# Attention's outputs turned and normalised on chip, V stored by pair, and a later sum of the experts in a hybrid encoder block

## The chip, the cores and the metric

The kernel runs on one core of one Trainium2 chip. The metric is the device time of one execution in microseconds (us), as the median of several runs; smaller is better. A profile comes from one further execution.

## The reference, cut to what matters

One layer over 1024 tokens of width 1024, all in float32. Tiles are 128 tokens, eight in all.

```python
n1 = modulate(h, norm1_g, sh1, sc1)
z, xbc, dtf, dtb, qkv, gate_ssd, gate_na = split(n1 @ w_in)
y_ssd = ssd_branch(z, xbc, dtf, dtb, ...) @ w_ssd_br
y_na = neighbourhood_attention(q, k, v, na_rpb) @ w_na_br
mixed = sigmoid(gate_ssd) * y_ssd + sigmoid(gate_na) * y_na
h = h + g1 * (mixed @ w_out)
n2 = modulate(h, norm2_g, sh2, sc2)
h = h + g2 * peer(n2, peer_wq, peer_keys, peer_u, peer_v)
return rms_norm(h, final_g)
```

The attention works on a grid of 16 rows of 64 tokens. A row's queries see 8 rows of keys (512 keys); 16 heads of 64 channels:

```python
s = einsum('qd,kd->qk', q, k) + bias      # 64 queries, 8 rows of keys, per head
o = einsum('qk,kd->qd', softmax(s), v)
```

`peer` picks for each token and each of 8 heads the 16 best of 16384 experts, which makes 128 rows of `peer_u` and 128 rows of `peer_v` (4 KB each) per token:

```python
act = gelu(einsum('thkd,td->thk', u[eidx], xc))
return einsum('thk,thkd->td', gate * act, v[eidx])
```

## The kernel before, in words

Every engine runs one fixed list of instructions, and semaphores tie the lists together. The stages are: the condition and the first norm, the projections (`stage_project`), v, z and gates (`stage_gates`), q and k (`stage_qk`), the recurrence (`stage_ssd`), and then `stage_tail`, which holds the rest: attention, the two branch products, the output product, the second norm, the queries and scores of the expert layer, and the expert layer itself.

`stage_tail` interleaves two things. The **stream** of the expert layer goes by slots, 128 per tile, one for each expert of each token: in slot n POOL fetches one row of `peer_u` for each of 128 tokens (512 KB, an indirect DMA, L2229) into a ring of 5 buffers, VectorE makes the dot product (L2397), and every 32 slots, a grain, make a unit: GELU (ScalarE, `GELU_AT`), weights (VectorE, L2346), a turn on TensorE (L2409), and a copy of the turned weights into the spread matrix `spread` (ScalarE, L2262). POOL also fetches the rows of `peer_v` (L2222, 512 KB each, a ring of 12 buffers), and TensorE sums them, four fetches a batch, with `spread` as weights into PSUM `acc` (L2443). A fetch into the ring of 12 waits for the sum three batches earlier. The constants `FETCH_AT` and `SUM_AT` say how many slots after a grain's end its fetches and sums begin.

The **lane** is the dense work. It runs in passes of two tiles; pass 0 comes before the stream, passes 1 to 3 are laid into the slots by a planner (`PE_COST` shares the slots, `GAP` leaves slots free ahead of a kind of job). A pass does, in this order: `gate` (loads `n1_scr`, six column blocks of `w_in`, L1680), `recur` (the recurrence), `attend`, `merge`, `prepare` (output product, second norm, queries, scores). Scores go to HBM, and SP loads them back `SCORES_LEAD` slots before the stream needs them (L2179).

`attend` handles 32 units in a pass (8 pairs of heads, 4 grid rows). A unit: scores of both heads in one product with a block-diagonal q (L1843), scale and bias (VectorE, L1945), row maximum (L1949), exp (ScalarE, L1878), four transposes on TensorE (L1860), copy to `PT` (ScalarE, L1872), four products with V (L1852), and a division by the row sums on the way out of PSUM (VectorE, L1960). The three parts of TensorE's work in one job belong to units `it`, `it - 2` and `it - 1`. The kept blocks go to HBM, `na_scr`, with 256-byte pieces (L1572), and are loaded back in `merge` and turned by TensorE before the product with `w_na_br`. V is loaded twice for each pair: once by tiles of 128 keys, once shifted by 64 keys, so that a unit whose window starts at an odd row finds its keys at partition 0:

```python
for b in range(4):
    last = nc.tensor.matmul(values_bank(a_pass, u), PT[:, u % 2, b, :],
                            V[:, p % RP, odd * nk + b0 + b, :], start=(b == 0), stop=(b == 3))
```

The names: `acc`, `ps_n2F`, `ps_l`, `ps_turn` are PSUM, `lane` and `ring` the shared SBUF areas, `lane<-n_scr` a load of `n1_scr`, `n<-n_scr` the load of `n2`.

## Time and profile before

| | us |
|---|---|
| median of 3 runs (4532.55 to 4545.38) | 4540.99 |
| the profiled execution, its own time | 4573.06 |
| its span | 4571.3 |
| first row of `peer_u` fetched | 1038.9 |
| last indirect fetch issued | 4552.1 |

Busy in the span: PE 2882.9, DVE 2629.4, ACT 777.6, POOL 2072.6. The 16 DMA engines moved 1443 MB. The profiled execution is 32 us longer than the median. A group of rows carries the time an engine was busy, the mean of one instruction, and the idle time just before it with what ended it. The DMA share is that of the time packets took, so it can exceed 1 a little.

### The profile page before, as it was taken

How to read it: one execution, taken by the hardware profiler on the slowest of the kernel's cores; microseconds unless marked ns; L12 is line 12 of the kernel's file. 1: busy time of each engine (PE TensorE's matmuls, PEld its weight loads, DVE VectorE, ACT ScalarE, POOL GpSimd, SP SyncE). 2: the span in 40 equal slices, each digit the busy share in tenths (PEclk: the TensorE clock that was granted, in tenths of full speed). 3: DMA queues.
4: the chain of work that ended last, by engine and by line, in shares of the span. 5: the costliest groups of instructions: out<-in, count | busy, mean ns of one | idle time of the engine just before them, and what ended most of it. 6: DMA issues, size and time to landing. Idle time of an engine off the chain costs nothing. (4 is left out here: it accounts for less than half of the span.)

```text
span 4571.3 us, 38523 instructions
## 1 busy us (share of the span) xinstructions
PE 2882.9 (63%) x12379; PEld 1502.5 (33%) x12379; DVE 2629.4 (58%) x5465; ACT 777.6 (17%) x1601; POOL 2072.6 (45%) x2154
## 2 busy tenths in 40 slices
PE   4989996895755666694466756944657573223334
PEld 3867775542222432331233223322332230000000
DVE  3862118427476756447677565467775656665652
ACT  3323222311122210111122101111221010000000
POOL 1000303004454455445645555456555556666665
PEclk8989998997877888897677878976778796555656
DMA  7544634448989999999999999989999999999998
GB/s 197 115 133 134 177 91 158 153 170 327 383 314 328 346 367 406 394 350 335 366 343 336 404 406 405 372 324 368 351 327 404 407 386 377 381 364 367 381 364 318
DMA packets 566934, 1442.97 MB, mean 316 GB/s; under 512 B 85416, under 2 KB 184720, under 8 KB 565712
## 3 DMA queue, kind: packets, MB, share of 16 engines
q0 software_dynamic: 298768, 1086.75, 63.5%
q1 hardware_dynamic: 267968, 353.77, 22.4%
q8 instruction: 101, 1.65, 0.1%
q14 instruction: 97, 0.79, 0.0%
HBM read 1364.96 MB, written 75.38 MB: 315 GB/s over the span
## 5 line engine op out<-in xcount | busy, mean ns | idle before, releaser
L2397 DVE CUSTOM_DVE_ANT_0 junkF<-ring,ps_n2F 128x1024 bf16<-128x1024 f32 x1024 | 1249.0, 1220 | 850.5 <-DMA ring<-in_peer_u,idx 568.3
L2229 POOL DMA_INDIRECT ring<-in_peer_u,idx x1024 | 983.7, 961 | 1251.3 <-DVE dots L2397 750.9
L2443 PE MATMUL acc<-ring,spread 128*32 128x512 f32 x4096 | 717.6, 817 | 913.1 <-DMA ring<-in_peer_v,idxT 681.8
L2222 POOL DMA_INDIRECT ring<-in_peer_v,idxT x1024 | 981.4, 958 | 551.5 <-issue 309.5
L1680 PE MATMUL ps_l<-lane 128*128 128x512 f32 x1856 | 864.1, 619 | 136.0 <-DMA lane<-n_scr 75.2
L2443 PEld LDWEIGHTS acc<-ring,spread 128*32 128x32 f32 x4096 | 146.7, 135 | 1375.7 <-issue 1289.5
L1680 PEld LDWEIGHTS ps_l<-lane 128*128 128x128 f32 x1856 | 355.7, 197 | 610.2 <-issue 579.0
L1852 PE MATMUL ps_l<-lane 128*128 128x128 f32 x768 | 146.4, 350 | 161.0 <-ACT lane L1872 125.5
L1852 PEld LDWEIGHTS ps_l<-lane 128*128 128x128 f32 x768 | 129.1, 251 | 241.7 <-ACT lane L1872 170.3
L1843 PE MATMUL ps_l<-lane 128*128 128x512 f32 x192 | 128.3, 756 | 81.3 <-DVE lane L1945 73.8
L717 POOL MEMSET colmask<- 128x64 f32 x1 | 0.2, 156 | 364.7 <-POOLq L604 364.7
L1723 PE MATMUL ps_l<-lane 128*128 128x512 f32 x96 | 83.2, 1017 | 100.5 <-DVE tok L1810 73.3
L1878 ACT ACTIVATE lane<-lane,nmax 128x512 f32<-128x512 f32 x96 | 69.3, 722 | 359.1 <-DVE nmax L1949 207.2
L1945 DVE SCALAR_TENSOR_TENSOR lane<-ps_l,lane 128x512 f32<-128x512 f32 x96 | 66.0, 687 | 90.6 <-DMA rpb_scr<-bias_pad 82.8
L773 DVE TENSOR_TENSOR w_qk_lo<-w_qk,w_qk_hi 128x1024 fp32r<-128x1024 f32 x16 | 24.9, 1558 | 153.6 <-ACT w_qk_hi L755 153.6
L567 PE MATMUL ps_x<-n_hi,w_x_hi 128*128 128x512 f32 x256 | 104.8, 409 | 11.3 <-DVE w_x_lo L447 11.3
L659 DVE TENSOR_TENSOR w_z_lo<-w_z,w_z_hi 128x512 fp32r<-128x512 f32 x64 | 40.7, 687 | 121.8 <-ACT w_z_hi L631 88.3
L567 PE MATMUL ps_qk<-n_hi,w_qk_hi 128*128 128x512 f32 x256 | 102.4, 400 | 9.9 <-DVE w_qk_lo L773 9.9
L2246 ACT ACTIVATE gatesF<-gatesF 128x16 f32<-128x16 f32 x64 | 13.2, 207 | 537.7 <-DVE gatesF L2330 318.1
L567 PE MATMUL ps_x<-n_lo,w_x_hi 128*128 128x512 f32 x256 | 103.1, 403 | 0.0
L567 PE MATMUL ps_x<-n_hi,w_x_lo 128*128 128x512 f32 x256 | 102.8, 402 | 0.0
L567 PE MATMUL ps_qk<-n_lo,w_qk_hi 128*128 128x512 f32 x256 | 102.2, 399 | 0.0
(327 smaller groups left out, 4054.0 us busy)
## 6 DMA issues: line engine op xcount, KB each, us to landing
lane<-in_w_in SPq DMA_DIRECT2D x18, 2048.0 KB
lane<-in_peer_wq SPq DMA_DIRECT2D x16, 2048.0 KB
adaB<-in_w_ada SPq DMA_DIRECT2D x16, 1024.0 KB
w_z<-in_w_in SPq DMA_DIRECT2D x16, 1024.0 KB
lane<-in_w_ssd_br SPq DMA_DIRECT2D x8, 2048.0 KB
lane<-in_w_na_br SPq DMA_DIRECT2D x8, 2048.0 KB
lane<-in_w_out SPq DMA_DIRECT2D x8, 2048.0 KB
ring<-in_peer_u,idx POOLq DMA_INDIRECT x1024
```

The costliest lines, as they stand in the source:

```text
L567: last = nc.tensor.matmul(bank, stationary(left, k), moving(right, k), start=(k == 0 and n == 0), stop=(k == KD - 1 and n == 2))
L659: nc.vector.tensor_tensor(parts[1][:, q % RP, :], w[:, k // KH, k % KH, :], parts[0][:, q % RP, :], ALU.subtract).then_inc(lo_done, 1)
L1680: last = nc.tensor.matmul(bank, inT[:, f % SETS, k, :], w[:, blk % RW, k, :], start=(k == 0), stop=(k == KD - 1))
L1723: nc.tensor.matmul(ps_a, masks[:, 2 + d, :], rhs[:, d, :, :].rearrange("p h n -> p (h n)"), start=(d == 0), stop=(d == 1))
L1843: nc.tensor.matmul(scores_bank(a_pass, u), qd[:, p % RP, i, :], kT[:, p % RP, k0:k0 + HALF], start=True, stop=True).then_inc(qk_done, 1)
L1852: last = nc.tensor.matmul(values_bank(a_pass, u), PT[:, u % 2, b, :], V[:, p % RP, odd * nk + b0 + b, :], start=(b == 0), stop=(b == 3))
L1878: nc.scalar.activation(S[:, u % 2, :], S[:, u % 2, :], ACT.Exp, bias=nmax[:, u % 2:u % 2 + 1], accum_out=rsum[:, u % 4:u % 4 + 1]).then_in ...
L1945: nc.vector.scalar_tensor_tensor(out=S[:, u % 2, :], in0=scores_bank(a_pass, u), scalar=HEADDIM ** -0.5, in1=bias[:, p % RP, s0:s0 + NA_KH ...
L2222: pool.indirect_dma_start(v_rows[:, nv % RV, :], None, a["peer_v"][0], bass.IndirectOffsetOnAxis(ap=idxT[:, m % 2, col:col + 1], axis=0)). ...
L2229: pool.indirect_dma_start(u_rows[:, n % RU, :], None, a["peer_u"][0], bass.IndirectOffsetOnAxis(ap=idx[:, i % RI, j:j + 1], axis=0)).then_ ...
L2397: nc.vector.tensor_tensor_reduce(out=junk[:, :], in0=u_rows[:, n % RU, :], in1=ps_n[:, :], scale=1.0, scalar=0.0, op0=ALU.mult, op1=ALU.ad ...
L2443: last = nc.tensor.matmul(acc[q * QUAD:(q + 1) * QUAD, cols], spread[:, c0:c0 + QUAD], v_rows[:, nv % RV, cols], start=(g == 0 and b == 0) ...
```

## The change

1. Attention's turn is a product with `diag`, the identity times the reciprocal of the row sums (made by VectorE one unit earlier than the division was), instead of a transpose with the identity. The product with V has V as the stationary operand, so it comes out turned; ScalarE copies its two kept 64x64 blocks straight into `inT`, the input of the product with `w_na_br`. `na_scr`, its stores, its loads and the turns of it are gone. The buffer O is gone.
2. V is stored as `v_scr[pair, key, tile, channel]` and loaded once. A unit with an odd first row takes two half tiles (64 keys) and three whole ones: five products in place of four, in the turn and in the product with V.
3. `merge` does the product with `w_na_br` first, `w_ssd_br` after it.
4. `spread` has two buffers; `FETCH_AT` 5 to 13, `SUM_AT` 8 to 16, so fetches and sums of a grain come 8 slots later after its end. `h` and `n2` share a buffer.
5. `SCORES_LEAD` 42 to 76. `GAP`: gate 3 to 10, y 4 to 3, ssd 4 to 3, na 4 (new).

```diff
-            sp.dma_start(V[:, p % RP, 0:nk, :], zg_scr[3, k0:k0 + nk * P, cols].rearrange("(t q) n -> q t n", q=P)).then_inc(done, 16)
-            sp.dma_start(V[:, p % RP, nk:, :], zg_scr[3, k0 + GRID_W:k0 + GRID_W + (nk - 1) * P, cols].rearrange("(t q) n -> q t n", q=P)).then_inc(done, 16)
+            sp.dma_start(V[:, p % RP, :, :], v_scr[p, :, KEY0[a_pass] // 2:KEY0[a_pass] // 2 + nk, :]).then_inc(done, 16)
...
-                for b in range(4):
-                    last = nc.tensor.matmul(values_bank(a_pass, u), PT[:, u % 2, b, :], V[:, p % RP, odd * nk + b0 + b, :], start=(b == 0), stop=(b == 3))
+                terms = [(slice(0, P), b, b0 + b) for b in range(odd, 4)]
+                if odd:
+                    terms = [(slice(GRID_W, P), 0, b0)] + terms + [(slice(0, GRID_W), 0, b0 + 4)]
+                for j, (keys, b, tile) in enumerate(terms):
...
+                    last = nc.tensor.matmul(values_bank(a_pass, u), V[keys, p % RP, tile, :], PT[keys, u % 2, b, :], start=(j == 0), stop=(j == len(terms) - 1))
...
                 pe.wait_ge(exp_done_a, g0 + u + 1)
+                pe.wait_ge(diag_done, g0 + u + 1)
...
-                for b in range(4):
-                    last = nc.tensor.transpose(turned_bank(a_pass, u)[:, b * P:(b + 1) * P], S[:, u % 2, b * P:(b + 1) * P], ident[:, :])
+                for b in range(odd, 4):
+                    c0 = b * P - odd * GRID_W
+                    last = nc.tensor.matmul(turned[:, b * P:(b + 1) * P], S[:, u % 2, c0:c0 + P], diag[:, u % 2, :], start=True, stop=True)
...
+                for hh in range(2):
+                    part = slice(hh * HEADDIM, (hh + 1) * HEADDIM)
+                    last = nc.scalar.activation(inT[part, f % SETS, p, i % 2 * GRID_W:(i % 2 + 1) * GRID_W], values_bank(a_pass, u)[part, part], ACT.Copy)
+                last.then_inc(o_done, 1)
...
+                nc.vector.tensor_scalar(diag[:, u % 2, :], ident[:, :], rinv[:, u % 2:u % 2 + 1], None, ALU.mult).then_inc(diag_done, 1)
...
-                v.wait_ge(pv_done, g + 1)
...
-                nc.vector.tensor_scalar(O[:, p % 2, i, :], values_bank(a_pass, u), rinv[:, u % 2:u % 2 + 1], None, ALU.mult).then_inc(o_done, 1)
...
-        FETCH_AT, SUM_AT = 5, 8
+        FETCH_AT, SUM_AT = 13, 16
...
-        ROUTE_LEAD, ROUTE_STEP, SCORES_LEAD = 36, 4, 42
+        ROUTE_LEAD, ROUTE_STEP, SCORES_LEAD = 36, 4, 76
...
-        GAP = dict(gate=3, sdec=LATE_SLOTS + 3, att=11, y=4, ssd=4, mix=2, n2=8, q=1)
+        GAP = dict(gate=10, sdec=LATE_SLOTS + 3, att=11, y=3, na=4, ssd=3, mix=2, n2=8, q=1)
...
-                            if m:
-                                act.wait_ge(v_used, m * BATCHES)
+                            if m >= 2:
+                                act.wait_ge(v_used, (m - 1) * BATCHES)
```

VectorE in the attention of pass 1. `lane<-ps_l,lane` is scores plus bias, `nmax` the row maximum, `rinv` the reciprocal; before:

```order
L2397 ISA dots 128x1
L1945 SCALAR_TENSOR_TENSOR lane<-ps_l,lane 128x512
L1949 TENSOR_REDUCE nmax<-lane 128x1
L1955 RECIPROCAL rinv<-rsum 128x1
L1960 TENSOR_SCALAR lane<-ps_l,rinv 128x128
L2339 RECIPROCAL grec<-gsum 128x2
```

and now:

```order
L2416 ISA dots 128x1
L1961 SCALAR_TENSOR_TENSOR lane<-ps_l,lane 128x512
L1967 RECIPROCAL rinv<-rsum 128x1
L1971 TENSOR_SCALAR lane<-ident,rinv 128x128
L1975 TENSOR_REDUCE nmax<-lane 128x1
L2416 ISA junkF,dots<-ring,ps_n2F 128x1024
```

The number of instructions is the same; the last one of a unit reads the identity in SBUF and not PSUM, waits for exp and not for the product with V, and stands ahead of the maximum.

TensorE where pass 2 begins with its gates. `ps_l<-keysT,qcol` are the last scores of pass 1, `acc<-ring,spread` the sums of the experts' rows (8 rows a batch), `ps_l<-lane` the first gate product; before:

```order
L1695 MATMUL ps_l<-keysT,qcol 128x128 x8
L2443 MATMUL acc<-ring,spread 32x512 x8
L1680 MATMUL ps_l<-lane 128x512 x4
L2443 MATMUL acc<-ring,spread 32x512 x8
L1680 MATMUL ps_l<-lane 128x512 x10
```

and now:

```order
L1682 MATMUL ps_l<-keysT,qcol 128x128 x8
L2462 MATMUL acc<-ring,spread 32x512 x24
L1667 MATMUL ps_l<-lane 128x512 x6
L2462 MATMUL acc<-ring,spread 32x512 x8
L1667 MATMUL ps_l<-lane 128x512 x12
```

Three batches of sums stand ahead of the first gate product, where one stood.

SP in the attention of pass 2, one pair of heads; before:

```order
L1572 DMA na_scr<-lane 64x4x64 x2
L1523 DMA lane<-qk_scr 64x4x64 x2
L1524 DMA lane<-qk_scr 128x768
L1525 DMA lane<-zg_scr 128x6x128
L1526 DMA lane<-zg_scr 128x5x128
L1527 DMA lane<-rpm_scr 128x512
```

and now:

```order
L1524 DMA lane<-qk_scr 64x4x64 x2
L1525 DMA lane<-qk_scr 128x768
L1526 DMA lane<-v_scr 128x768
L1527 DMA lane<-rpm_scr 128x512
L2197 DMA qs<-score_scr 128x512
```

The two stores are gone, and V is one load with long pieces.

## Rows read from the trace of the kernel before

**Rows 1.** The page: engines, and the rate of the DMA engines in 40 slices.
```profile
PE 2882.9 (63%) x12379; PEld 1502.5 (33%) x12379; DVE 2629.4 (58%) x5465; ACT 777.6 (17%) x1601; POOL 2072.6 (45%) x2154
...
GB/s 197 115 133 134 177 91 158 153 170 327 383 314 328 346 367 406 394 350 335 366 343 336 404 406 405 372 324 368 351 327 404 407 386 377 381 364 367 381 364 318
```

**Rows 2.** By stretches: length, PE, PEld, DVE, ACT, POOL busy, clock, DMA share, GB/s.
```profile
1490.00:1660.00 170.00, 109.16 (x574) 61.39 (x565) 123.26 (x287) 41.80 (x101) 89.35 (x93) 0.79 0.96 340
...
1930.00:2150.00 220.00, 151.04 (x554) 61.30 (x554) 113.94 (x253) 35.10 (x74) 102.69 (x108) 0.81 0.93 349
...
2300.00:2530.00 230.00, 138.60 (x716) 78.17 (x716) 166.74 (x390) 50.19 (x115) 124.65 (x132) 0.78 0.95 341
2530.00:2850.00 320.00, 225.21 (x864) 92.63 (x864) 185.18 (x403) 40.16 (x87) 175.42 (x183) 0.85 1.03 405
2850.00:2980.00 130.00, 111.02 (x368) 42.27 (x368) 60.04 (x135) 15.39 (x26) 63.95 (x68) 0.90 0.98 376
...
3110.00:3440.00 330.00, 189.96 (x990) 102.69 (x990) 238.21 (x545) 67.81 (x158) 183.22 (x193) 0.76 0.96 346
...
3763.00:4505.00 742.00, 238.26 (x1156) 53.80 (x1160) 447.60 (x987) 36.81 (x90) 491.11 (x516) 0.60 0.97 373
```

**Rows 3.** DMA issues of the whole span: count and KB of each.
```profile
lane<-zg_scr SPq DMA_DIRECT2D x16, 384.0 KB
lane<-zg_scr SPq DMA_DIRECT2D x16, 320.0 KB
...
tok<-na_scr SPq DMA_DIRECT2D x8, 512.0 KB
...
na_scr<-lane SPq DMA_DIRECT2D x48, 64.0 KB
...
lane<-zg_scr SPq DMA_DIRECT2D x8, 256.0 KB
...
lane<-zg_scr SPq DMA_DIRECT2D x8, 192.0 KB
```

**Rows 4.** SP's queue, 1700 to 2000 us: packets, MB, share.
```profile
q1 hardware_dynamic: 16797, 31.88, 28.2%
```

**Rows 5.** The same, 2200 to 2500 us.
```profile
q1 hardware_dynamic: 22704, 14.82, 16.6%
```

**Rows 6.** TensorE in pass 0: two parts of a unit, and the end.
```profile
805.68 0.60 PE L1860 MATMUL acc<-ident,ring 128*128 128x128 f32 x4
...
807.69 1.16 PE L1852 MATMUL ps_n2F<-ring 128*128 128x128 f32 x8 [0.55 <-ACT ring L1872]
...
893.11 3.65 PE L1668 MATMUL ps_l<-ident,tok 128*128 128x128 f32 x16 [7.10 <-DMA tok<-y_scr]
```

**Rows 7.** Waits from 1400 to 3763 us: total, times, longest.
```profile
DVE best L2281 <- DMA qs<-score_scr: 69.1, 7, 17.9
...
DVE lane L1960 <- remote: 27.2, 8, 4.9
DVE lane L1960 <- PE ps_l L1852: 25.8, 22, 5.1
```

**Rows 8.** Waits from 1900 to 2000 us, where pass 2 begins.
```profile
PE ps_l L1680 <- DMA lane<-n_scr: 29.6, 1, 29.6
POOL ring L2222 <- PE acc L2443: 25.2, 2, 22.8
DVE junkF L2397 <- ACT ps_n2F L2241: 21.7, 1, 21.7
```

**Rows 9.** ScalarE and TensorE near 3994 us, instructions in order.
```profile
3993.56 0.94 ACT L2262 ACTIVATE spread<-ps_turn 32x32 f32<-32x32 f32 x4 [41.15 <-remote]
3994.55 5.40 PE L2443 MATMUL acc<-ring,spread 128*32 128x512 f32 x32 [28.18 <-ACT spread L2262]
```

**Rows 10.** VectorE in pass 0, two instructions of a unit.
```profile
804.90 0.69 DVE L1945 SCALAR_TENSOR_TENSOR ring<-ps_l,ring 128x512 f32<-128x512 f32 x1 [0.95 <-PE ps_l L1843]
...
806.48 0.35 DVE L1960 TENSOR_SCALAR ring<-ps_l,rinv 128x128 f32<-128x128 f32 x1
```

More of the change, by code:

```diff
@@ L1368, in stage_tail @@
             kind = job[0]
-            if kind == "load" or (kind == "turn" and job[3] == 0):
-                t = job[1] if kind == "load" else job[2]
-                tile_set[t] = len(set_last)
-                set_last.append(None)
-                set_ready.append(None)
-                set_jobs.append(n)
+            if kind in ("load", "open") or (kind == "turn" and job[3] == 0):
+                for t in PASSES[job[1]] if kind == "open" else [job[1] if kind == "load" else job[2]]:
+                    (value_set if kind == "open" else tile_set)[t] = len(set_last)
+                    set_last.append(None)
+                    set_ready.append(None)
+                    set_jobs.append(n)
             if kind == "load":
@@ L1418, in stage_tail @@
                     gin_jobs.append(n)
-                if what == "na":
+                if what == "ssd":
                     mix_job[c, t] = n
@@ L1449, in tok_loads @@
         def tok_loads(g):
-            return sum(1 for i in range(g + 1) if i % RT == g % RT and tok_kind[i][0] in ("y", "na"))
+            return sum(1 for i in range(g + 1) if i % RT == g % RT and tok_kind[i][0] == "y")
         def tok_norms(g):
@@ L1539, in load_late @@
                 sp.wait_ge(p_mm, last_before[t // 2] + 1)
+                for i in range(MIX):
+                    sp.wait_ge(s_keep[i], 16 * (t // 2))
             else:
@@ L1602, in sp_job @@
                         load_gin(sp, g)
-            if kind == "turn" and n in tok_of and JOBS[n][3] == 1:
-                g = tok_of[n] + RT
-                if g < len(tok_kind) and tok_kind[g][0] == "na":
-                    load_tok(sp, g)
             if kind == "turn" and JOBS[n][1] == "mix" and JOBS[n][3] == 1:
@@ L1699, in scores_bank, with odd_units @@
             return (acc if a_pass == 0 and u % 2 else ps_l)[:, 0:HALF]
+        def odd_units(a_pass, u):
+            return sum((first_row[ROWS[p][k % len(ROWS[p])]] - KEY0[p]) % 2 for p in range(a_pass + 1) for k in range(u if p == a_pass else ALL_UNITS[p]))
         def values_bank(a_pass, u):
@@ L1844, in pe_attend @@
             u = it - 2
-            if part == 1 and u >= 0:
+            if part == 1 and 0 <= u < units:
                 p, i = divmod(u, nr)
@@ L2036, in _ @@
                 sp.dma_start(final_g[:, :], a["final_g"].partition_broadcast(P)).then_inc(s_end_rows, 16)
+                for g in range(RT):
+                    load_tok(sp, g)
                 for blk in range(RW):
```

160 lines of the change are left out of this document (84 added, 76 removed).

## The prediction

> **What bounds the kernel now.** I read the page first, for the share of each engine. No engine is full: TensorE 63%, VectorE 58%, POOL 45%, ScalarE 17% [rows 1]. From slice 10 to the end, that is from the start of the stream, the DMA engines move 314 to 407 GB/s [rows 1]. The view by stretches has their share of busy time there at 0.93 to 1.03 [rows 2]. So the transfers bound three quarters of the span, but not at one rate: in the merge of pass 2 the engines move 405 GB/s without a dip, in attention 340, 341 and 346, at the beginnings of passes 2 and 3 349 and 376, and behind the last pass, where only the stream is left, 373 [rows 2]. I take 405 as what the engines give to this mix, and call the rest dead time: length times (1 - rate / 405). It is 27, 36 and 48 us in the three attentions (111 together), 30 and 9 at the two beginnings, 59 behind the last pass. In a stretch at 405 GB/s only bytes and packets count; in the others also who waits for whom. Ahead of the stream, the first 1039 us, DMA is idle much of the time, and TensorE's and VectorE's chains decide.
>
> **Step 1, fewer bytes and packets in passes 1 to 3.** Removed [rows 3]: 48 stores of 64 KB in 256-byte pieces (3.1 MB, 12288 packets); six of the eight loads of the same data (3.1 MB, 768 packets; the other two are pass 0's); of V 16 x 704 KB and 8 x 448 KB become 16 x 384 and 8 x 256 KB (15.2 to 8.4 MB), and pieces of 512 bytes become pieces of 2 to 3 KB (29696 to 3072 packets). That is 13.1 MB and 39680 packets. What a packet costs apart from its bytes I fit from two stretches of SP's queue: 28.2% of 16 engines in 300 us are 1354 us for 16797 packets and 31.88 MB [rows 4]; 16.6% are 797 us for 22704 packets and 14.82 MB [rows 5]. Two equations give 36.5 us per MB and 11.3 ns per packet. The saving is (13.1 x 36.5 + 39680 x 0.0113) / 16 = 30 + 28 = **58 us**, if nothing but the engines bounds these stretches. The lower bound is 0, the upper 58 and no more. I take it whole, because of that share. The stores of V in four times as many pieces fall in a stage where the rate is below 180 GB/s (slices 3 to 6 [rows 1]), so I cost them at nothing; without that cover 16 x 384 more packets would be 4 us.
>
> **Step 2, the beginning of a pass.** At the start of pass 2 TensorE stands 29.6 us for the load of `n1_scr`; behind it in its list are the sums, so POOL waits 22.8 us for a buffer of the ring of 12, and ScalarE is late with the tile's `n2`, for which VectorE, and with it the ring of 5, stands 21.7 us [rows 8]. The change leaves 10 slots and not 3 ahead of the first gate product. A slot of this part is 220 us over 54 (108 POOL instructions, two a slot [rows 2]), 4.1 us, so 7 slots are 29 us, about the wait. Bounds: nothing (the load is late again) to 39 us (both dead times). I take **28 us**, near the upper end since three batches of sums now stand ahead of the product.
>
> **Step 3, attention inside the stream.** 28 of the 111 us of dead time are the small packets of step 1. VectorE waits 27.2 + 25.8 = 53 us in L1960 for the product with V [rows 7], and the dot products queue behind it, so POOL's ring of 5 too. That wait goes: `diag` needs exp of the unit before, done a unit (two slots) earlier. VectorE's own count is the same. ScalarE gets two more copies a unit, 0.24 us each by the spread's four in 0.94 us [rows 9], and is 17% busy; hidden. TensorE gets more: a product of this size, four of them, takes 1.16 us and the transposes 0.60 us [rows 6], so a unit costs 0.56 us more, 54 us in 96 units, and the 32 odd units another 2 x 0.29 us each, 19 us; 12 turns of four transposes go (0.6 us each, 7 us). TensorE is busy 57 to 64% in these stretches [rows 2], so cycles are there; but the turn now also waits for `diag`, which VectorE makes in the same slot, behind dot products that wait for DMA. Sums queue behind it. Bounds: a gain of 40 us (half of 53 shows, and some of the rest goes) to a loss of 40. I take a gain of **10 us**.
>
> **Step 4, the sums 8 slots later, two spread matrices.** Near 3994 us ScalarE's copy into `spread` comes late, and TensorE stands 28.2 us for it [rows 9]; POOL then lacks a buffer of the ring of 12, as it did at the start of pass 2 [rows 8]. Before, the copy had two slots until the first sum and needed all sums of the grain before; now it has ten slots and needs those of two grains before. In the last stretch a slot is 742 / 258 = 2.9 us, so 23 us more: a delay like this is just hidden. Next in line is POOL itself, which needs 2 x 0.95 us and its issue for each slot. Of the 59 us of dead time I take a third, **20 us**, since the wait shown is the largest of its kind and most are shorter; bounds 0 and 45. The later fetches leave 8 more of them behind the last row of `peer_u` (about 1.3 us each) and 8 fewer before: +1 us.
>
> **Step 5, scores 34 slots earlier.** VectorE waits 69 us for them in all, 17.9 us at most [rows 7]. But such a wait in a stretch that already runs at 405 GB/s costs no DMA time, since weights fill it. I take **5 us**; bounds 0 and 15.
>
> **Step 6, pass 0.** It lies ahead of the stream, with nothing to hide in. TensorE idles there 0.55 us in two units [rows 6], that is 0.28 a unit, and a unit costs 0.56 more: 32 x 0.28 to 32 x 0.56, 9 to 18 us. The load of y (7.1 us of idle TensorE [rows 6]) is now made at the start, and four turns (about 2 us) go. I take 15 - 9 = **+6 us**; bounds -5 and +25. The Trainium skill speaks against this step: its page "TensorE: Matmul & The Clock Gate", in Terms, says that TensorE's transpose mode is four times faster for FP32, and the change gives the mode up. By it the four products would take 4 x 0.60 = 2.4 us, 1.24 us more than the like product takes, and pass 0 would lose some 40 us on top, an estimate from that page. No row shows a transpose's place taken by a product; the nearest row prices the same shape at 1.16 [rows 6], and I go by it. The other 96 units would lose it in TensorE's slack.
>
> **The sum.** -58 -28 -10 -20 -5 +6 +1 = -114 us. Against the profiled execution's 4573.1 that is 4459; it is 32 us longer than the median, so against 4541.0 it is **4427 us**. A measurement of this kernel can tell about 0.3%, 14 us, from no change.
>
> **The rivals.**
> (a) *Only bytes go, the waits move.* The engines are in-order lists, and a wait taken from VectorE comes back at the next one. For it: the three attentions run at almost the same rate though their V differs. Against it: the merge stretches show that 405 GB/s can be held with the same lists. Time: 4541 - 58 + 7 = 4490.
> (b) *More of the dead time goes.* The six stretches have 209 us of it, 181 beside the packets; my steps 2 to 5 take 63. If two thirds go, 121, the time is 4541 - 58 - 121 + 7 = 4369. Against it: each stretch has waits that the change leaves, such as those of the recurrence.
> (c) *The turn ties TensorE to VectorE.* This one ends slower. In each unit of passes 1 to 3 TensorE holds its list until VectorE has done scores, reciprocal and `diag`, and VectorE's next unit needs TensorE's next scores. Price if nothing hides it: 0.69 + 0.35 us on VectorE [rows 10] and 0.56 more on TensorE, 1.6 us a unit, in 96 units 154 us; the sum without step 3 is -104, so 4591. It decides from 104 / 96 = 1.1 us a unit. Against it: a unit has two slots, over 7 us.
> (d) *The turn is dearer than the product with V.* If the four products took four times the transposes' 0.60 us [rows 6], pass 0, which alone is bound by TensorE, would pay 32 x (2.4 - 1.16) = 40 us more: 4467, and with sums that come late behind dearer turns some 4480. This is the ratio that the Trainium skill gives in the page and section named in step 6. Against it: before, four products of this shape took twice the transposes' time.
> (e) *The freed DMA time isn't used.* POOL's fetch of a row waits until VectorE has freed one of 5 buffers, so if the ring's depth and not the engines' rate sets the pace, fewer packets elsewhere give nothing: 4541 + 7 = 4548. Against it: in the merge stretch the same ring fills 405 GB/s.
>
> **How the numbers follow.** Forecast (4385 to 4480) 0.54; (a) 0.20; (b) 0.12; (c) 0.05; (d) 0.04; (e) 0.05. The predicted time is the forecast's, 4427. The range takes in (a) and (d) and the larger part of (b): 4350 to 4510. Left out are (c), (e) and the rest of (b), and tails of the forecast. Faster by over 0.3% are forecast, (a), (b) and (d): 0.90; within it (e): 0.05; slower (c): 0.05.
>
> **What would show it right or wrong.** Step 1: attentions above 350 GB/s, fewer packets below 512 bytes and below 2 KB, and the stream faster there. Step 2: the wait of TensorE for `lane<-n_scr` under 10 us. Step 3: no wait of VectorE in the `diag` line worth naming; wrong if TensorE's turn waits for VectorE by more than 1 us a unit. Step 4: no wait of TensorE for `spread` in the last stretch and a grain there below 90 us. Step 6: the first fetch of `peer_u` at 1045, within 1030 to 1065 us; past 1080 it is (d). The prediction as a whole is wrong if the merge stretches fall below 390 GB/s, or if the attentions stay at 345 with their packets gone.

## The result, and the profile after

| | before | after | ratio, 95% interval |
|---|---|---|---|
| median of 14 runs each, us | 4550.47 | 4526.52 | 0.9941 (0.9929 to 0.9954) |
| profiled execution, us | 4573.06 | 4505.74 | |

The change gains 24 us by the medians, 27 by the ratio; forecast were 114, with a range of 4350 to 4510 us. The sign was right, the size wrong by a factor of four to five. The two profiled executions differ by 67 us, since that of before is slower than all 14 of its runs and that of after faster than the 13 others: they show where time goes, not how much the change is worth.

The page of the changed kernel, its engines and the rate by slices (as [rows 1]):

```profile
PE 2969.7 (66%) x12955; PEld 1567.6 (35%) x12955; DVE 2610.1 (58%) x5465; ACT 818.4 (18%) x1837; POOL 2079.6 (46%) x2154
...
GB/s 196 113 140 128 183 86 146 145 154 279 388 293 368 318 352 404 398 403 357 351 369 316 402 407 405 403 351 352 350 320 403 407 400 383 362 379 375 374 382 325
```

The stretches that answer to [rows 2], with the same columns: the attentions of passes 1, 2 and 3 are the first, third and sixth, the beginnings of passes 2 and 3 the second and fifth, the last is behind all passes:

```profile
1490.00:1660.00 170.00, 133.52 (x682) 76.39 (x682) 118.06 (x279) 47.48 (x132) 85.54 (x89) 0.83 0.88 318
1910.00:2110.00 200.00, 137.25 (x529) 53.62 (x522) 110.51 (x249) 31.64 (x68) 109.18 (x116) 0.83 1.02 398
2270.00:2500.00 230.00, 165.12 (x922) 96.15 (x920) 163.66 (x390) 63.51 (x183) 124.51 (x131) 0.84 0.92 344
2500.00:2810.00 310.00, 224.40 (x861) 93.60 (x865) 179.12 (x384) 34.04 (x76) 171.42 (x178) 0.84 1.03 405
2810.00:2940.00 130.00, 111.76 (x368) 42.45 (x360) 65.06 (x152) 17.38 (x28) 70.09 (x75) 0.89 1.03 404
3060.00:3380.00 320.00, 203.94 (x1108) 118.38 (x1109) 231.79 (x541) 78.24 (x218) 178.83 (x188) 0.78 0.93 336
3695.00:4430.00 735.00, 249.30 (x1168) 55.59 (x1168) 447.52 (x984) 36.79 (x90) 493.10 (x516) 0.59 0.97 377
```

The merge still runs at 405 GB/s. The two beginnings rose from 349 and 376 to 398 and 404: that dead time is gone. The rate in the attentions did not rise: 318, 344 and 336, where 340, 341 and 346 stood, and the share of the DMA engines' time fell from 0.96, 0.95, 0.96 to 0.88, 0.92, 0.93. The engines have less to do there and stand more. By the forecast's own sign ("if the attentions stay at 345 with their packets gone") it is wrong as a whole. The attentions did get shorter: from the first to the last sum of scores (L1945, now L1961) the three take 609 us in the trace before and 570 in this one; the experiments show how much of that is the settings'. The last stretch has 377 for 373.

The traffic is as counted: from 1055 us to the end SP's queue went from 150752 to 109824 packets and from 213.23 to 200.12 MB, 40928 packets and 13.1 MB less, where step 1 had 39680 and 13.1. Its packets take 16.8% of the 16 engines' time there before and 15.6% now, that is 591 and 539 us: 52 us less, where step 1 had 58. V's loads, and the page's line on packets for the whole span, pass 0 included (before: 566934 packets, 1442.97 MB):

```profile
DMA packets 521245, 1426.27 MB, mean 317 GB/s; under 512 B 67369, under 2 KB 138001, under 8 KB 520017
...
lane<-v_scr SPq DMA_DIRECT2D x16, 384.0 KB
...
lane<-v_scr SPq DMA_DIRECT2D x8, 256.0 KB
```

The waits from 1400 to 3695 us that answer to [rows 7] (L1961 is scores plus bias, L1848 the product with V, L2300 the first use of loaded scores):

```profile
DVE lane L1961 <- DMA adaB<-in_w_ada: 71.8, 17, 6.4
PE ps_l L1848 <- ACT lane L1888: 61.0, 24, 7.1
...
DVE lane L1961 <- PE ps_l L1834: 53.4, 27, 5.5
...
DVE best L2300 <- DMA qs<-score_scr: 40.3, 3, 16.6
```

VectorE no longer waits for the product with V. It waits in the next instruction that needs TensorE, the scores' sum, 125 us. Before, that wait was shorter (1400 to 3763 us):

```profile
DVE lane L1945 <- DMA rpb_scr<-bias_pad: 82.8, 24, 5.9
DVE lane L1945 <- PE ps_l L1843: 4.5, 5, 1.1
```

With the 53 us in L1960 that is 140 before and 125 now: most of the wait has moved. The releasers named, a load of `w_ada` and one of `bias_pad`, belong to the first stages, so they can't be the true ones; such a row says only that the profile doesn't know what released the wait. The wait for loaded scores fell from 69.1 to 40.3 us. TensorE's wait for `lane<-n_scr`, 29.6 us in one piece in [rows 8], is down to 10.7 us over the whole stretch. In the line of `diag` VectorE doesn't wait; TensorE's turn waits for `diag` 13.2 us in three places.

TensorE in pass 0 (as [rows 6]), where the turn of a unit is now L1862 (a float32 product leaves two records, a transpose one, so x8 is four products):

```profile
804.25 1.13 PE L1862 MATMUL ps_l<-ring 128*128 128x128 f32 x8
805.21 1.02 PE L1834 MATMUL ps_l<-ring 128*128 128x512 f32 x2
806.60 1.16 PE L1848 MATMUL ps_l<-ring 128*128 128x128 f32 x8 [0.36 <-ACT ring L1888]
807.59 1.06 PE L1862 MATMUL acc<-ring 128*128 128x128 f32 x8
```

Four products of 128x128 take 1.06 to 1.16 us, as priced, and the first row of `peer_u` is fetched at 1043.3 us, 4.4 us later than before.

### The profile page after: what moved, and what is told of

It is laid out like the page before. It is cut to its first block, busy times and chain, and to the rows that moved or that the text cites. A ratio compares the mean times of both kernels' runs of the same rounds, so it can differ in the third digit from the quotient of the medians.

```text
span 4503.8 us, 39785 instructions
## 1 busy us (share of the span) xinstructions
PE 2969.7 (66%) x12955; PEld 1567.6 (35%) x12955; DVE 2610.1 (58%) x5465; ACT 818.4 (18%) x1837; POOL 2079.6 (46%) x2154
## 4 chain that ended last, share of the span: by engine, by line
DMA 18%; issue 16%; PE 14%; DVE 13%; POOL 11%; another core or an unknown queue 4%; ACT 1%; SPq 0%; DVEq 0%; POOLq 0%; ACTq 0%
DMA ring<-in_peer_u,idx 11%; PE ps_l L1667 6%; POOL ring L2248 6%; POOL ring L2241 5%; DVE junkF L2416 5%; DMA ring<-in_peer_v,idxT 3%; PE acc L2462 2%; DMA gin<-zg_scr 1%; PE ps_l L1848 1%; PE ps_l L1714 1%; PE ps_l L1862 1%; PE ps_l L1834 1%; DMA lane<-zg_scr 1%; DMA lane<-n_scr 1%
## 5 line engine op out<-in xcount | busy, mean ns | idle before, releaser
L1667 PEld LDWEIGHTS ps_l<-lane 128*128 128x128 f32 x1856 | 360.7, 200 | 584.9 <-issue 557.3
L1848 PE MATMUL ps_l<-lane 128*128 128x128 f32 (+1 forms) x832 | 151.5, 327 | 86.2 <-ACT lane L1888 61.0
L1848 PEld LDWEIGHTS ps_l<-lane 128*128 128x128 f32 (+1 forms) x832 | 126.4, 221 | 170.3 <-ACT lane L1888 99.3
L1862 PE MATMUL ps_l<-lane 128*128 128x128 f32 x704 | 122.0, 323 | 57.9 <-issue 44.5
L1961 DVE SCALAR_TENSOR_TENSOR lane<-ps_l,lane 128x512 f32<-128x512 f32 x96 | 66.1, 688 | 137.1 <-DMA adaB<-in_w_ada 71.8
L1862 PEld LDWEIGHTS ps_l<-lane 128*128 128x128 f32 x704 | 105.0, 226 | 78.8 <-issue 74.2
```

The lines of the kernel that those rows point to most:

```text
L1667: last = nc.tensor.matmul(bank, inT[:, f % SETS, k, :], w[:, blk % RW, k, :], start=(k == 0), stop=(k == KD - 1))
L1848: last = nc.tensor.matmul(values_bank(a_pass, u), V[keys, p % RP, tile, :], PT[keys, u % 2, b, :], start=(j == 0), stop=(j == len(terms) - 1))
L1862: last = nc.tensor.matmul(turned[:, b * P:(b + 1) * P], S[:, u % 2, c0:c0 + P], diag[:, u % 2, :], start=True, stop=True)
L1961: nc.vector.scalar_tensor_tensor(out=S[:, u % 2, :], in0=scores_bank(a_pass, u), scalar=HEADDIM ** -0.5, in1=bias[:, p % RP, s0:s0 + NA_KH ...
```

## The experiments

The experiments ran on five chips, and every ratio is against the kernel before on the same chip. The chips turned out to be of two kinds. On two of them the kernel before takes 4413 and 4414 us (the **faster** kind), on three 4568 to 4574 (the **slower** kind, to which the chip of the result with 4550 belongs by its traces). The 3.5% between them are more than the change, and parts of the change have different signs on the two:

| kernel | faster chips | slower chips |
|---|---|---|
| after | | 0.9941, 0.9933 |
| att_alone, att_alone_b | 0.9877 | 1.0022 |
| rest_alone, rest_alone_b | 1.0023 | 0.9973 |
| slots_back, slots_back_b | 0.9907, 0.9914 | |
| gate3 | 0.9900 | |
| lead76 | | 1.0033 |
| sums_later | | 1.0034 |
| lead42 | | 0.9995 |
| traffic_back | | 1.0057 |
| turn_by_product | | 1.0051 |
| before_ring6 | 0.9973 | |
| after_ring6, after_ring6_b | 0.9873 | 0.9872 |
| att_slot_later | 0.9880 | |
| ring6_slot_later | | 0.9836 |

The 95% intervals reach 0.0012 to 0.0024 to either side. The changed kernel itself never ran on a faster chip, and slots_back and gate3 never on a slower one.

### Attention alone, and the settings alone

att_alone is the changed kernel with the three new settings at their old values:

```diff
-        FETCH_AT, SUM_AT = 13, 16
+        FETCH_AT, SUM_AT = 5, 8
-        ROUTE_LEAD, ROUTE_STEP, SCORES_LEAD = 36, 4, 76
+        ROUTE_LEAD, ROUTE_STEP, SCORES_LEAD = 36, 4, 42
-        GAP = dict(gate=10,
+        GAP = dict(gate=3,
-                            if m >= 2:
-                                act.wait_ge(v_used, (m - 1) * BATCHES)
+                            if m:
+                                act.wait_ge(v_used, m * BATCHES)
```

> The changed kernel with the old settings: fetches and sums at 5 and 8, spread written after the sums of the grain before, scores 42 slots ahead, 3 slots ahead of the gates. What is left is attention, V and the new merge. Measured for the whole change: 0.594% less, 27 us. Theory W (waits move inside attention: VectorE's wait for the product with V comes back as a wait for the scores' product, and the freed DMA time isn't used): ratio 0.998 to 1.003. Theory B (the bytes and packets gave the 27 us and the settings gave nothing): 0.992 to 0.996. Theory C (bytes give the forecast 58 us and the settings take 30 back): 0.985 to 0.990.

Measured 4359.32 against 4413.41 us, 0.9877 (0.9859 to 0.9896): 54 us, on a faster chip.

The new gaps of `merge` and the recurrence (y 3, ssd 3, na 4) stay in, so "attention alone" includes them. In every run whose `SCORES_LEAD` is 42 the score parts start two slots after the load again, as before; the fences leave that line out.

rest_alone is the kernel before with these settings at their new values, two spread matrices and `h` in the buffer of `n2`:

```diff
-        h = sb("h", [P, DM])
         n2 = sb("n2", [P, DM])
+        h = n2
-        spread = sb("spread", [P, (GRAIN + 1) * QUAD])
+        spread = sb("spread", [P, 2, (GRAIN + 1) * QUAD])
-        FETCH_AT, SUM_AT = 5, 8
+        FETCH_AT, SUM_AT = 13, 16
-        ROUTE_LEAD, ROUTE_STEP, SCORES_LEAD = 36, 4, 42
+        ROUTE_LEAD, ROUTE_STEP, SCORES_LEAD = 36, 4, 76
-        GAP = dict(gate=3,
+        GAP = dict(gate=10,
```

> The kernel before with the new settings alone: two spread matrices, h in n2's buffer, fetches and sums at 13 and 16, scores 76 slots ahead, 10 slots ahead of the gates; attention as before. Theory W: 0.993 to 0.996, nearly the whole gain. Theory B: 0.998 to 1.002. Theory C: 1.004 to 1.008.

Measured 4424.84 us, 1.0023 (1.0010 to 1.0035): a loss of 10 us on the same chip, half of what theory C had for it. The traces of the two in the attention of pass 2, 2240 to 2440 us; first rest_alone, which has the old attention, then att_alone (columns as in [rows 2]):

```profile
2240.00:2440.00 200.00, 127.71 (x662) 65.74 (x663) 150.04 (x350) 48.07 (x108) 110.58 (x118) 0.80 1.03 381
```

```profile
2240.00:2440.00 200.00, 154.68 (x904) 87.51 (x903) 160.25 (x382) 65.39 (x183) 126.16 (x133) 0.88 1.03 395
```

With both, the DMA engines are busy all the time (share 1.03). Fewer packets and bytes of the lane let POOL do 133 operations in the place of 118. The three attentions take 554 us with the old form and 509 with the new. From 1055 us to the end the packets of SP's queue take 17.5% of the 16 engines' time in rest_alone and 16.3% in att_alone, 590 and 538 us, again 52 less. So step 1's price of the traffic is some 10% high and no more. The 54 us are those of steps 1, 3 and 6 together, for which the forecast had 62; how much of them is the traffic's was not measured, since the run that puts the traffic back (below) fell on a slower chip.

### The same two on a slower chip

> Attention's new form alone, again, with the three new settings at their old values. On a chip where the kernel before took 4413 us it gave 0.9877; on one where it takes 4574 us, one setting more gave 1.0033 and the removed traffic put back 1.0057. Theory 'the gain is the DMA engines' time on every chip': 0.986 to 0.990 here too. Rival 'on a chip of the slower kind, where POOL stands in short stops that the faster one doesn't show, fewer bytes give little': 0.995 to 1.003.

> The kernel before with all the new settings and none of attention's new form, again. It gave 1.0023 where before took 4413 us. Theory 'the settings help only where the stops are': on the slower kind of chip 0.988 to 0.994, on the faster 1.002 again. Rival 'the settings cost on every chip': 1.002 here too. My steps 2, 4 and 5 (53 us) would give 0.988.

att_alone_b gave 4582.0 against 4572.69 us, 1.0022 (1.0006 to 1.0038): no gain but a loss of 10 us, as the rival in its expectation had it. rest_alone_b gave 0.9973 (0.9957 to 0.9989), a gain of 12 where its theory had 27 to 55. The attention of pass 2, first in rest_alone_b (old form), then in att_alone_b (new form):

```profile
2280.00:2480.00 200.00, 132.03 (x667) 70.04 (x660) 148.71 (x348) 49.55 (x113) 104.17 (x110) 0.78 0.98 355
```

```profile
2290.00:2490.00 200.00, 149.87 (x818) 89.14 (x818) 137.38 (x333) 59.62 (x162) 101.76 (x108) 0.84 0.89 326
```

The same program that had 395 GB/s there on the faster chip has 326, at a share of 0.89 for 1.03. Against the old form on the same chip the share fell by 0.09 and POOL did 108 operations for 110. From 1055 us on SP's queue takes 595 us of the engines in rest_alone_b and 545 in att_alone_b, so the traffic is 50 us cheaper on this kind of chip too; the time isn't used. So on this chip the transfers don't bound the attention, and taking them away doesn't help by itself.

VectorE's waits for the scores from 1400 to 3695 us, first in att_alone_b, then in att_alone:

```profile
DVE lane L1961 <- DMA adaB<-in_w_ada: 116.7, 26, 6.5
DVE lane L1961 <- PE ps_l L1834: 48.7, 25, 5.5
```

```profile
DVE lane L1961 <- PE ps_l L1834: 44.2, 30, 2.7
```

On the slower chip the wait is 165 us and more than the 140 of before; on the faster chip it is 44. The three attentions together show where the parts act:

| three attentions, us | faster chips | slower chips |
|---|---|---|
| old form, old settings | | 609 (before) |
| old form, new settings | 554 (rest_alone) | 575 (rest_alone_b) |
| new form, old settings | 509 (att_alone) | 620 (att_alone_b) |
| new form, new settings | | 570, 575 (after, after_again) |

On the faster chip the new form shortens them by 45 us. On the slower ones the settings shorten them by 34 and the new form by nothing beyond that.

### What the slower chips show that the quick ones don't

The cleanest place is the last stretch, where only the stream runs. POOL's waits from 3720 to 4350 us, in the changed kernel on a slower chip (after_again):

```profile
POOL ring L2241 <- issue: 64.7, 199, 2.4
POOL ring L2248 <- issue: 60.4, 196, 0.9
POOL ring L2241 <- remote: 56.1, 17, 5.6
POOL ring L2248 <- DVE dots L2416: 23.6, 21, 9.3
POOL ring L2241 <- PE acc L2462: 9.4, 2, 4.8
```

and in gate3, nearly the same kernel, on a faster one:

```profile
POOL ring L2241 <- issue: 77.7, 255, 0.4
POOL ring L2248 <- issue: 53.3, 175, 0.3
POOL ring L2248 <- DVE dots L2416: 36.6, 44, 3.6
POOL ring L2241 <- PE acc L2462: 5.8, 5, 4.1
```

The row "remote" (a releaser that the profile doesn't know) is on the slower chip alone. Over the span POOL has 46 such stops, 124 us; the kernel before has 39, 113.5 us; the faster chips' traces have none. One stop in detail, POOL in after_again:

```profile
3816.24 0.94 POOL L2241 DMA_INDIRECT ring<-in_peer_v,idxT  x1 [0.30 <-issue]
3817.49 0.94 POOL L2248 DMA_INDIRECT ring<-in_peer_u,idx  x1 [0.30 <-issue]
3823.99 0.94 POOL L2241 DMA_INDIRECT ring<-in_peer_v,idxT  x1 [5.55 <-remote]
```

TensorE's sum before it had ended at 3817.36, and VectorE too stands in these microseconds, 3.12 us with the same label. The DMA rate in slices of 1 us from 3800 us on:

```profile
GB/s 418 393 410 418 414 401 406 418 410 401 414 410 418 401 410 406 422 397 414 406 422 401 287 78 20 74 250 299 295 356 295 217 336 340 410 401 414 426 414 422
```

From 4 us after POOL's stop begins the engines run empty, down to 20 GB/s. Stops of 56 us in 630 are 9%, and the stretch runs at 370 GB/s there against 404 in gate3, 8% less. So the dead time that I had read as waits of TensorE for `spread` goes, in this stretch, with these stops. The whole last stretch bears that out: from the fetch of slot 768 to the last one it takes 669 to 671 us in every trace of a faster chip and 725 to 741 in every one of a slower chip, whatever the change. POOL's stops from 3720 to 4500 us sum to 65 to 88 us in the slower chips' traces, enough for those 54 to 72. What they are the profile doesn't say. The program's instructions take the same time on both chips (a dot product 1.22 us), and up to the start of the stream there is no difference (first fetch 1047.6 us in att_alone, 1045.3 in att_alone_b): all the stops lie in the stream, where the DMA engines are loaded. In the passes the stops of POOL don't account for the rest: att_alone_b is 223 us longer than att_alone, and POOL's stops in it sum to 104. ScalarE and VectorE have rows with the same label there; what makes up the rest, and what causes the stops, stays open. Whether other users of the chip do was not tried.

### The changed kernel and its settings, one by one

On the faster chip, the changed kernel with the old slots and the old wait for the spread matrix (slots_back), and with the old gate gap (gate3):

```diff
-        FETCH_AT, SUM_AT = 13, 16
+        FETCH_AT, SUM_AT = 5, 8
-                            if m >= 2:
-                                act.wait_ge(v_used, (m - 1) * BATCHES)
+                            if m:
+                                act.wait_ge(v_used, m * BATCHES)
```

> The changed kernel with fetches and sums at 5 and 8 and the one-grain wait of the spread copy again. Step 4 of the prediction had 20 us for them: ratio 0.998 to 0.999 against before if it holds (the whole change 0.994 plus 0.0044). If the delay of the spread copy was hidden by the ring of 12 anyway: 0.993 to 0.995.

```diff
-        GAP = dict(gate=10,
+        GAP = dict(gate=3,
```

> The changed kernel with 3 slots ahead of the first gate product in place of 10. Step 2 had 28 us for them: ratio 0.999 to 1.001 against before if it holds. If the 7 slots are only taken from attention and the products behind, and the wait moves there: 0.993 to 0.996.

Measured 0.9907 (0.9889 to 0.9925) and 0.9900 (0.9880 to 0.9919), below all that their expectations had, since those were reckoned from a slower chip's 0.994: two settings on top of att_alone take back 10 to 13 us of its 54.

On slower chips, the changed kernel again, then attention's new form with one or two settings:

> The changed kernel once more, so that it and its parts are compared on one chip. Attention's new form alone gave 0.9877 of the kernel before, with 2 of the 3 new settings 0.990. Theory 'settings cost' (each of gate gap, later sums, earlier scores takes something back): 0.991 to 0.995, as 0.9941 on the first chip. Rival 'it was the first chip' (the settings' loss shows only there, where the pure stream runs at 373 GB/s): 0.987 to 0.990.

lead76 is slots_back and gate3 together (the wait of slots_back belongs to it, cut here):

```diff
-        FETCH_AT, SUM_AT = 13, 16
+        FETCH_AT, SUM_AT = 5, 8
-        GAP = dict(gate=10,
+        GAP = dict(gate=3,
```

> Attention's new form with one setting, scores loaded 76 slots ahead; gate gap and sums as before. Both runs that had this setting lay at 0.990. If it is the scores' lead that costs: 0.990 or above. If the cost lies in the gate gap or the later sums: 0.987 to 0.9885. My forecast was a gain of 5 us by it, 0.9866.

sums_later takes the changed kernel's lead and gap back:

```diff
-        ROUTE_LEAD, ROUTE_STEP, SCORES_LEAD = 36, 4, 76
+        ROUTE_LEAD, ROUTE_STEP, SCORES_LEAD = 36, 4, 42
-        GAP = dict(gate=10,
+        GAP = dict(gate=3,
```

> Attention's new form with one setting, fetches and sums 8 slots later and two spread matrices. Theory 'on the slower kind of chip this setting hides the stops' (TensorE waits for the spread matrix there, not on the faster kind): there 0.990 to 0.994, clearly below attention alone; on the faster kind 0.988 to 0.990, no gain. Rival 'the gain there is the gate gap's': here the same as attention alone.

and lead42 the lead alone:

```diff
-        ROUTE_LEAD, ROUTE_STEP, SCORES_LEAD = 36, 4, 76
+        ROUTE_LEAD, ROUTE_STEP, SCORES_LEAD = 36, 4, 42
```

> The changed kernel with the scores loaded 42 slots ahead as before; gate gap 10 and later sums stay. The changed kernel gave 0.9933 to 0.9941 on two chips of the slower kind. If the scores' lead costs: 0.987 to 0.991. If it gives the 5 us forecast: 0.994 to 0.996. If it decides nothing: 0.992 to 0.995.

Measured: after_again 0.9933 (0.9909 to 0.9956); the scores' lead alone (lead76) 1.0033 (1.0013 to 1.0054); later sums alone (sums_later) 1.0034 (1.0017 to 1.0052); later sums and gate gap (lead42) 0.9995 (0.9982 to 1.0008). From att_alone_b's 1.0022 one gets: later sums nothing (+5 us, within the intervals); with the gate gap 0.4% less, 18 us, on the same chip; with the earlier scores another 0.6% less, 28 us, where the two runs are on different slower chips. Alone (lead76 against att_alone_b, on two chips) the scores' lead gives nothing; it gains once the gate gap and the later sums are there. Which of the two it needs is not shown: the lead and the gap without the later sums ran only on faster chips, so a part of the 28 us may be the later sums'. The expectation of lead42 that the lead gives 5 us (0.994 to 0.996) failed: without it the gain is gone.

The steps also depend on their order. With the old settings the new attention costs 10 us on a slower chip; with the new ones it gains about 18 (after_again's 0.9933 against rest_alone_b's 0.9973, on two chips). The settings give 12 us with the old attention and about 40 with the new.

### The traffic put back

att_alone with V stored by token and loaded twice in pieces of 512 bytes, the second time for nobody, and the stores to `na_scr` made of a constant (the edit is cut: it also adds a buffer and waits to SP's list):

```diff
+            sp.dma_start(again[:, 0:nk - 1, :], zg_scr[3, k0 + GRID_W:k0 + GRID_W + (nk - 1) * P, cols].rearrange("(t q) n -> q t n", q=P)).then_inc(s_again, 16)
...
+                        sp.dma_start(v_scr[t0:t1, c0:c0 + HEADDIM].rearrange("(r q) n -> q r n", q=GRID_W),
+                                     final_g[part, 0:4 * HEADDIM].rearrange("p (r n) -> p r n", r=4)).then_inc(s_dummy, 16)
```

> Attention's new form alone, with the removed traffic put back: V stored by token and loaded in 512-byte pieces, the shifted second load of V into a buffer that nobody reads, and the stores to na_scr of the same size and pieces (of a constant); only the loads of na_scr (3 MB) stay out. Theory 'the gain is the DMA engines' time' (58 us, less 7 for the loads that stay out): the gain of 54 us all but goes, 0.997 to 1.001. Rival 'the gain is the waits' (VectorE's wait for the product with V, the turns in the merge): it stays, 0.988 to 0.991. Half of each: 0.993 to 0.995.

Measured 1.0057 (1.0037 to 1.0077), on a slower chip, outside all that was expected, which went by a faster chip's 0.9877. Against att_alone_b's 1.0022 (another slower chip) that is 0.35%, 16 us, with intervals that allow some 4 to 28, for traffic that step 1 prices at about 50 and that takes 43 us of the engines' time (588 us for SP's queue from 1055 us on, 545 in att_alone_b). Of the 16, 4.6 us lie ahead of the stream (first fetch 1049.9 us for 1045.3). On the faster chip it wasn't tried.

### The turn as a product

The kernel before with the four transposes of a unit written as products with the identity:

```diff
-                    last = nc.tensor.transpose(turned_bank(a_pass, u)[:, b * P:(b + 1) * P], S[:, u % 2, b * P:(b + 1) * P], ident[:, :])
+                    last = nc.tensor.matmul(turned_bank(a_pass, u)[:, b * P:(b + 1) * P], S[:, u % 2, b * P:(b + 1) * P], ident[:, :], start=True, stop=True)
```

> The kernel before with attention's four transposes of a unit made products with the identity. A product was 0.56 us dearer per four than the transposes. Theory of step 6 (pass 0 pays 9 to 18 us, the stream hides the rest): 1.002 to 1.004. Rival 'the stream pays too' (128 units x 0.56 = 72 us): 1.012 to 1.016. Rival 'the turn is four times dearer' (1.8 us a unit in pass 0): 1.010 or above with the first fetch 50 us later.

Measured 1.0051 (1.0032 to 1.0070), 23 us. In its profiled execution the first fetch comes at 1046.1 us and not at 1038.9, 7 us later. The other 16 us or so are lost inside the stream, where TensorE had seemed to have room. The result lies between my two expectations: pass 0 pays, and the stream pays 16 of the 54 us that 96 units cost more.

### A sixth buffer, and attention's work a slot later

slots_back_b is slots_back again. after_ring6 is the same with one spread matrix and the 4 KB of the other as a sixth buffer for rows of `peer_u`; before_ring6 does it to the kernel before, with `h` in the buffer of `n2`:

```diff
-    RU, RV, RI = 5, 12, 2
+    RU, RV, RI = 6, 12, 2
-        spread = sb("spread", [P, 2, (GRAIN + 1) * QUAD])
+        spread = sb("spread", [P, 1, (GRAIN + 1) * QUAD])
```

> The changed kernel with fetches and sums at their old slots and the spread matrix awaited as before, again, now for the slower kind of chip. Theory 'the gate gap with the earlier scores is what gains there, the later sums nothing' (attention alone 1.0022, later sums alone 1.0034): 0.992 to 0.996, like the changed kernel. Rival 'the later sums give the gain, once the gates are out of the way' (step 4's 20 us): 0.997 to 1.000. On a chip of the faster kind 0.9907 again.

> The changed kernel with one spread matrix (fetches and sums 5 and 8 slots after a grain, as before), and the 4 KB of the second one used as a sixth buffer of the ring of peer_u. Theory 'a stop of an engine becomes lost DMA time because the ring holds 5 rows' (rival (e) of the prediction): at least 40 us below the same kernel with 5 buffers (slots_back_b), so 0.984 or less on a slower chip. Rival 'VectorE, not the ring, is late': within 10 us of slots_back_b. On a chip of the faster kind, where DMA is never idle, both say: no change from 0.9907.

> The kernel before with h and n2 in one buffer and the room used as a sixth buffer of the ring of peer_u; nothing else. Theory 'the ring of 5 sets the pace on the slower kind of chip': 0.975 to 0.990 there. Rival 'it does not': 0.997 to 1.001. On a chip of the faster kind: 0.995 to 1.000 for both.

All three ran on one faster chip: 0.9914 (0.9895 to 0.9933), 0.9873 (0.9853 to 0.9894), 0.9973 (0.9961 to 0.9986). The sixth buffer is worth 15 us in the changed kernel and 10 in the kernel before; in the kernel before that includes `h` moved to the buffer of `n2`. I had expected nothing in the changed kernel on such a chip.

att_slot_later is the changed kernel with VectorE's and ScalarE's part of a unit one slot later:

```diff
-                    slot = max(slot, part_slot[n, 1])
+                    slot = max(slot, part_slot[n, 1] + 1)
```

> The changed kernel with attention's work of VectorE and ScalarE one slot later against TensorE's. VectorE waited 125 us in pass 1 to 3 for the product of scores and its data (90 us before the change). Theory 'this wait took the place of the one removed and costs dead time': 5 to 20 us less than the changed kernel, 0.990 to 0.993 on a slower chip. Rival (c) 'the turn ties TensorE to VectorE': TensorE now stands for exp and diag, 10 to 60 us more, 0.996 to 1.006. If neither counts: 0.993 to 0.995.

Measured 0.9880 (0.9860 to 0.9900) on the faster chip, where its expectation had numbers for a slow one only. It has no reference with the same settings there; the nearest is slots_back_b, 13 us above it.

> The changed kernel with one spread matrix, old slots of fetches and sums, and a sixth buffer of the ring of peer_u, again. On a chip of the faster kind it gave 0.9873, 18 us below the same with 5 buffers. Theory 'the ring of 5 turns stops into lost DMA time on the slower kind': 0.976 to 0.988 there. Rival 'it doesn't matter there': 0.992 to 0.997, as the changed kernel. On a faster chip 0.987 again.

> after_ring6_b with attention's work of VectorE and ScalarE one slot later. Theory 'VectorE's wait for the product of scores costs dead time': 5 to 15 us below after_ring6_b. Rival 'with six buffers the wait is hidden': within 4 us of it. Rival (c) 'TensorE then stands for diag': 10 us or more above it.

Both ran on one slower chip (before: 4567.98 us). after_ring6_b gave 4508.56 us, 0.9872 (0.9857 to 0.9887), which lies in the range of the first theory, 28 us below the 0.9933 of the changed kernel on another slower chip. That is the buffer and the old slots of fetches and sums together; slots_back didn't run on a slower chip, so they aren't told apart. ring6_slot_later gave 4497.42 us, 0.9836 (0.9814 to 0.9857): another 11 us. VectorE's waits for the scores from 1400 to 3695 us, in after_ring6_b:

```profile
DVE lane L1961 <- DMA adaB<-in_w_ada: 75.5, 17, 8.0
DVE lane L1961 <- PE ps_l L1834: 68.1, 36, 5.7
```

and in ring6_slot_later:

```profile
DVE lane L1961 <- DMA adaB<-in_w_ada: 69.6, 18, 6.5
DVE lane L1961 <- PE ps_l L1834: 41.0, 30, 5.6
```

33 us of VectorE's waiting go, and 11 of the time. The last stretch stays as it was (370 GB/s, POOL's "remote" 68.5 us): the sixth buffer doesn't hide a stop of POOL itself. That it helps where VectorE was late is likely but not shown. ring6_slot_later beats the kernel before by 1.6% on its chip, and the changed kernel by about 1% across two chips.

## Why the prediction was wrong

**What bounds the kernel.** I took a share of 0.95 and a rate of 345 GB/s as an engine bound by transfers with a little dead time. On a chip like the result's it isn't: in the attentions the DMA engines ran empty for moments, and the cause was not in the byte count. The tell was in my own rows: the stretch of merge showed that the same lists can hold 405, and two of the waits that I priced, 27.2 us in [rows 7] and 41.15 in [rows 9], carry the label "remote".

**Step 1, -58 us, is the step that failed.** Its price of the traffic was nearly right: SP's queue takes 50 to 52 us less of the engines' time on both kinds of chip, where 58 were reckoned, and on the faster one, where the DMA share in the attention is 1.03, steps 1, 3 and 6 gave 54 of 62 us. What failed is the term's other half, that this time comes off the kernel's. On a slower chip att_alone_b shows +10 in place of the forecast -62 (steps 1, 3 and 6), and the traffic itself is worth some 16. The clause "if nothing but the engines bounds these stretches" was the condition, I took the upper bound as the value, and it doesn't hold there. This is the outcome of rival (e), the freed time isn't used, for two thirds of the step or more; its mechanism, the depth of the ring, is not shown to be the cause. I had given it 0.05, from the merge's 405 GB/s, which tells of another stretch.

**Step 2, -28, and step 5, -5, held in their places, and together gave more than forecast once the new attention was in.** The beginnings of passes 2 and 3 run at 398 and 404 GB/s; gate gap and scores' lead give 18 and 28 us in the runs. Step 5 was too small: the lead gives nothing alone and 28 us with gap and later sums, and I had priced each singly. With the old attention steps 2, 4 and 5 gave 12 of their 53 us.

**Step 3, -10.** The wait for V's product went, and VectorE's waiting at the scores rose from 87 to 125 us, so rival (a) describes it: of 140 us in the two places 15 went. Moving the work by a slot recovers 11 us of that. Rival (c) with its 1.6 us a unit did not come, yet turn_by_product shows that a dearer turn costs some 16 us in the stream of the kernel before, which I had put down as hidden.

**Step 4, -20, gave nothing in its stretch.** The forecast read one wait of 28 us for `spread` as the pattern of the last stretch. TensorE's waits for it are gone in the profile after, and the stretch has 377 GB/s for 373. Waits from 3763 to 4505 us, before:

```profile
PE acc L2443 <- ACT spread L2262: 74.0, 5, 28.2
POOL ring L2222 <- remote: 64.6, 18, 6.1
```

and POOL's from 3695 to 4430 us, after:

```profile
POOL ring L2241 <- issue: 75.4, 239, 2.2
POOL ring L2241 <- remote: 73.8, 19, 5.6
```

All 74 us of TensorE's waiting for `spread` went, and the last fetch came 725 us after that of slot 768, where it had come 733 after. The stops without a known releaser, 64.6 us before and 73.8 after, are what is left there, and the faster chips, which have none, run the stretch in 671 us; a row of POOL's waits there was in reach before the prediction. Whether the later sums gain elsewhere, with the scores' lead, is open as said above.

**Step 6, +6.** The first fetch came 4.4 us later here, and 6 to 12 us later in the other traces of the new attention. Rival (d), four times the transposes' 0.60 us, is out: the turn by product takes 1.06 to 1.16 us. The Trainium skill, "TensorE: Matmul & The Clock Gate", Terms, gives the transpose mode four times the speed for FP32; here it has 1.8 to 1.9 times the product's (0.60 us against 1.06 to 1.16).

**The sum on slower chips**, from the runs in this order: attention +10, later sums +5, gate gap -18, earlier scores -28, together -31. It ends at after_again's -31 by the way it is made, over two chips, so it is no test; on the chip of the result the change measured -24 to -27. That the sign came out as forecast is partly luck: with the old settings the new attention alone is a loss on these chips.

## What to carry to other kernels

In this kernel fewer bytes gave time where the DMA share was at 1, and little where it stood at 0.95 with short dips. So price the condition of an upper bound, not the bound. Before removing traffic, ask for the feeder's own waits in that stretch (here POOL's), and for waits whose releaser the profile doesn't know. On the slower chips one buffer more in the feeder's ring with the sums at their old slots gained 28 us, and a consumer moved one slot away from its producer 11 more; 13 MB of traffic gained some 16. On a faster chip the buffer gained 15 us, and the new attention with its 13 MB less 54. So measure the parts on more than one chip, and in more than one order.

## What the runs showed of the hardware

- The same program takes 4413 us on some chips and 4568 to 4574 on others, 3.5% apart. The slower ones show stops of POOL of up to 6.1 us with an unknown releaser, 34 to 50 in a trace, all of them in the stream; in the last stretch they are long enough for the whole difference (54 to 72 us); over the span they come to about half of it (104 of 223 us for the new attention). Their cause is open. A change can gain on one kind and lose on the other: 0.9877 and 1.0022 for the new attention, 1.0023 and 0.9973 for the settings.
- On the faster chips the pure stream holds 398 to 405 GB/s at a DMA share of 1.00 to 1.02, while POOL issues two operations of 1.25 us (0.94 busy and 0.30 of issue) in a slot of 2.6 us (1.05 MB at 404 GB/s): the two limits are some 5% apart, an estimate from these numbers.
- A product of 128x128 in float32 with the identity costs 1.8 to 1.9 times the transpose of that size, 0.27 to 0.29 us against 0.15.
